# Expert rows on their way to the tokens: plain f32 in two column halves in place of f32r high and low parts

## What is computed

```python
def expert_block(args):
    tok, gte, e = args
    xb = x_pad[tok]
    hb = jax.nn.silu(xb @ w1[e]) * (xb @ w3[e])
    return (hb @ w2[e]) * gte[:, None]
...
y = jnp.zeros((n + 1, d)).at[slot_tok].add(y_slots.reshape(n_slots, d))
```

## Time and profile before

| | us |
|---|---|
| median of 3 runs | 1051.43 (1050.07 to 1052.33) |
| the profiled execution | 1051.55 |
| its span, first to last instruction | 1049.8 |
| PE busy | 997.7 (95%) |
| DVE busy | 503.1 (48%) |
| ACT busy | 343.2 (33%) |
| chain that ended last | PE 75%, DMA 13%, DVE 6% |
| HBM read | 259.60 MB |

### The profile page before, as it was taken

The page is one execution under the profiler, slowest core; times in us unless marked ns, Lnnn a source line. Parts: engine busy times, 40 slices in busy tenths (PEclk is TensorE's granted clock), DMA queues, the critical chain, the costliest instruction groups (busy, mean ns, idle before and its releaser), DMA issues.

```text
span 1049.8 us, 12592 instructions
## 1 busy us (share of the span) xinstructions
PE 997.7 (95%) x4901; PEld 629.3 (60%) x4901; DVE 503.1 (48%) x915; ACT 343.2 (33%) x684; POOL 41.9 (4%) x59
## 2 busy tenths in 40 slices
PE   8999999999999999999997999999999889898894
PEld 7778867766778889877786344444343333333342
DVE  5369799765466445532336333333332232333236
ACT  6442365667763245443232211111111110111113
POOL 1000000000000000000000100000000000000001
PEclk9999999999999999999997999999999999999998
DMA  8422312112113626322278999999999999999992
GB/s 238 130 81 81 120 41 81 41 42 80 41 45 117 234 87 198 123 81 86 73 327 312 381 429 426 427 427 426 426 426 425 429 425 429 425 428 426 426 406 90
DMA packets 64431, 260.72 MB, mean 248 GB/s; under 512 B 11329, under 2 KB 39026, under 8 KB 50802
## 3 DMA queue, kind: packets, MB, share of 16 engines
q1 hardware_dynamic: 59954, 248.08, 59.6%
q0 software_dynamic: 3104, 7.35, 1.9%
q10 hardware_dynamic: 1312, 4.46, 1.2%
HBM read 259.60 MB, written 4.19 MB: 251 GB/s over the span
## 4 chain that ended last, share of the span: by engine, by line
PE 75%; DMA 13%; DVE 6%; issue 3%; ACT 1%; SPq 0%; DVEq 0%; POOLq 0%
PE ps L1958 16%; DMA eraw<-in_w 12%; PE ps L1649 12%; PE ps L1650 12%; PE ps L1651 12%; PE ps L2011 8%; PE ps L2022 2%; PE ps L2023 2%; PE ps L1884 1%; PE ps L1906 1%; PE ps L1826 1%; PE ps L1834 1%; DVE s L1273 1%; DVE nmax L1275 1%; PE ps L1852 1%
## 5 line engine op out<-in xcount | busy, mean ns | idle before, releaser
L1958 PE MATMUL ps<-eraw,XT 128*64 128x512 f32 x992 | 225.9, 598 | 12.8 <-DMA eraw<-in_w 11.6
L1224 DVE TENSOR_TENSOR wlo<-raw,whi 128x2048 fp32r<-128x2048 f32 (+2 forms) x43 | 95.9, 2230 | 115.6 <-ACT whi L906 115.5
L1958 PEld LDWEIGHTS ps<-eraw,XT 128*64 128x64 f32 x992 | 67.4, 136 | 133.7 <-issue 129.5
L2011 PE MATMUL ps<-eraw,HT 128*64 128x512 f32 x512 | 113.0, 593 | 8.2 <-issue 8.2
L1518 DVE TENSOR_TENSOR h<-ps,h 128x512 f32<-128x512 f32 x128 | 79.4, 684 | 82.8 <-PE ps L2023 82.8
L1649 PE MATMUL ps<-xT_hi,whi 128*128 128x512 f32 (+1 forms) x256 | 104.0, 406 | 1.6 <-DVE xT_lo L1231 1.6
L1650 PE MATMUL ps<-xT_lo,whi 128*128 128x512 f32 (+1 forms) x256 | 100.0, 391 | 0.0
L1651 PE MATMUL ps<-xT_hi,wlo 128*128 128x512 f32 (+1 forms) x256 | 100.0, 390 | 0.0
L906 ACT ACTIVATE whi<-raw 128x2048 fp32r<-128x2048 f32 (+2 forms) x43 | 80.1, 1864 | 45.5 <-PE ps L1651 45.3
L2011 PEld LDWEIGHTS ps<-eraw,HT 128*64 128x64 f32 x512 | 39.4, 137 | 79.9 <-issue 79.9
L1064 ACT ACTIVATE HT<-ps 128x512 f32<-128x512 f32 x15 | 9.0, 598 | 197.7 <-PE ps L1996 197.7
(11 more groups left out here) (316 smaller groups left out, 1577.4 us busy)
## 6 DMA issues: line engine op xcount, KB each, us to landing
eraw<-in_w SPq DMA_DIRECT2D x82, 2048.0 KB, 29.1
eraw<-in_w SPq DMA_DIRECT2D x28, 1024.0 KB, 10.8
raw<-in_w_in SPq DMA_DIRECT2D x9, 1024.0 KB, 5.2
raw<-in_w_gate SPq DMA_DIRECT2D x8, 1024.0 KB, 5.4
raw<-in_w_ckv SPq DMA_DIRECT2D x8, 1024.0 KB, 5.3
raw<-in_w_out SPq DMA_DIRECT2D x4, 1024.0 KB, 5.2
raw<-in_w_cq SPq DMA_DIRECT2D x4, 1024.0 KB, 5.1
raw<-in_w_co SPq DMA_DIRECT2D x4, 1024.0 KB, 5.0
```

The source lines that it names most:

```text
L1224: dve.tensor_tensor(wlo[n % 2][:, 0:w], raw[n % RING][:, 0:w], whi[n % 2][:, 0:w].bitcast(f32), ALU.subtract).then_inc(w_lo, 1)
L1958: ins = pe.matmul(ps[1 + c // 2][rows, :], XT[p % 2][:, kk, rows], eraw[slot][:, first + 512 * k:first + 512 * k + 512], start=(kk == 0), ...
L2011: ins = pe.matmul(ps[4 + n][rows, :], HT[:, ff, rows], eraw[slot][:, first + D * f + 512 * n:first + D * f + 512 * n + 512], start=(ff == ...
```

## The change

`Yh` and `Yl` give way to one tile `Y` in f32, and S becomes f32 as well. ACT's copy of the two banks writes `Y`; DVE's subtraction `rest` goes. A combine becomes two plain f32 matmuls: the first takes the stationary columns of tokens 0 to 63 of the tile and writes partitions 0 to 63 of the bank, the second tokens 64 to 127 and partitions 64 to 127; both stream the same 512 columns of `Y`. PE's waits for `yl_kept` become waits for `y_kept`, which ACT raises. In the branch for experts with too many tokens DVE gets a wait for `y_kept`.

```diff
-    Yh = at("Yh", [P, D], f32r, R_C)
-    Yl = at("Yl", [P, D], f32r, R_C, 32 * KB)
-    S = at("S", [P, SEQ], f32r, R_C, 39 * KB)
+    Y = at("Y", [P, D], f32, R_C)
+    S = at("S", [P, SEQ], f32, R_C, 39 * KB)
...
-                    act.activation(Yh[:, 512 * n:512 * n + 512], ps[4 + n][:, :], ACT.Copy).then_inc(yh_kept, 1)
+                    act.activation(Y[:, 512 * n:512 * n + 512], ps[4 + n][:, :], ACT.Copy).then_inc(y_kept, 1)
...
-            def rest(p):
-                for n in (0, 1):
-                    dve.wait_ge(yh_kept, 2 * p + n + 1)
-                    c = slice(512 * n, 512 * n + 512)
-                    dve.tensor_tensor(Yl[:, c], ps[4 + n][:, :], Yh[:, c].bitcast(f32), ALU.subtract).then_inc(yl_kept, 1)
...
-                if p:
-                    rest(p - 1)
...
-            rest(NPAIR - 1)
...
             def combine(t, n, bank):
-                o = ps[bank][:, :]
                 c = slice(512 * n, 512 * n + 512)
-                pe.matmul(o, S[:, P * t:P * t + P], Yh[:, c], start=True, stop=False)
-                pe.matmul(o, S[:, P * t:P * t + P], Yl[:, c], start=False, stop=True).then_inc(comb_made, 1)
+
+                for half in (0, 1):
+                    rows = slice(P // 2 * half, P // 2 * half + P // 2)
+                    ins = pe.matmul(ps[bank][rows, :], S[:, P * t + P // 2 * half:P * t + P // 2 * half + P // 2], Y[:, c],
+                                    start=True, stop=True)
+                ins.then_inc(comb_made, 1)
...
-                pe.wait_ge(yl_kept, 2 * p + 2)
+                pe.wait_ge(y_kept, 2 * p + 2)
...
-                pe.wait_ge(yl_kept, 2 * (NPAIR - 1) + n + 1)
+                pe.wait_ge(y_kept, 2 * (NPAIR - 1) + n + 1)
```

More of the change, by code:

```diff
@@ L501, in build @@
     sg_done, gg_done, h_done, turned, ht_kept = sem("sg_done"), sem("gg_done"), sem("h_done"), sem("turned"), sem("ht_kept")
-    y_half, yh_kept, yl_kept, s_done = sem("y_half"), sem("yh_kept"), sem("yl_kept"), sem("s_done")
+    y_half, y_kept, s_done = sem("y_half"), sem("y_kept"), sem("s_done")
     comb_made, comb_added = sem("comb_made"), sem("comb_added")
@@ L1502, in owned @@
                 dve.wait_ge(s_done, 2 * p + 1)
-                dve.scalar_tensor_tensor(S[:, :], slot_row[:, 1, :], slots, S[:, :].bitcast(f32),
+                dve.scalar_tensor_tensor(S[:, :], slot_row[:, 1, :], slots, S[:, :],
                                          ALU.is_equal, ALU.add).then_inc(s_done, 1)
-            def rest(p):
-                for n in (0, 1):
-                    dve.wait_ge(yh_kept, 2 * p + n + 1)
-                    c = slice(512 * n, 512 * n + 512)
-                    dve.tensor_tensor(Yl[:, c], ps[4 + n][:, :], Yh[:, c].bitcast(f32), ALU.subtract).then_inc(yl_kept, 1)
             def add_one(no, t, n, bank):
@@ L1574, in far_link @@
                     dve.wait_ge(over_chain, far_links[0])
+                dve.wait_ge(y_kept, 2 * NPAIR)
                 dve.wait_ge(comb_added, NC * (NPAIR - 1))
```

## The result

The changed kernel takes 1067.97 us (median of 4 runs, 1066.6 to 1069.26) against 1051.87 us before (4 runs): a ratio of 1.0159, 95% interval 1.0145 to 1.0173, 16.1 us slower. The forecast was 1068.7 us, 0.7 above the median.

The account below looks back on a forecast made before the run. PE was taken to set the pace throughout, the weight loads' 18.5 us lead keeping it from running dry. 12.75 (pairs) + 3.0 (last pair) + 1.4 (end) = 17.15 us on 1051.55 gave 1068.7 us, range 1064 to 1077.

Parts of the forecast that it names:

- The price of a combine: PE's combines: two plain f32 matmuls, 4 records, 0.859 us each; a pair's eight take 6.87 us in place of 4.08.
- The entries: 0.15 us once per stretch of 64-column records after full-array work on PE; two of four a pair go, 0.30 us off.
- The pair and the 14 pairs: PE's time of a pair goes from 27.07 to 29.56 us; down projection of pair 14 ends 12.75 us later.
- The last pair and the end: Last pair's two stretches of combines cost +3.0 us; last eight combines and adds +1.4, the bound moving from DVE to PE.
- the pairs up to 774 us had no wait to fill: Explanation of +12.75 us: later added PE work replaces waits for weights; earlier pairs have none, so their loss stays.
- A later release of weight places: Weight loads: places freed later delay loads that have 18.5 us of lead; put at nothing.
- A: Rival: the loads hide it all; only last pair and end cost, +4.4 us, 1055.9 us; chance 0.04.
- B: Rival: both halves share one stream of Y, a combine costs 0.43 us; -1.2 us, 1050.4 us; chance 0.03.
- C: Rival: the halves run one after the other, a combine costs 1.72 us; 1178.6 us; chance 0.04.
- D: Upper bound as a case: entries stay everywhere, a pair takes 30.15 us; 1077.4 us; chance 0.07 with what lies between.

Follow-up runs that it names:

- e1: Changed kernel with each combine as one whole plain f32 matmul over all 128 columns, no halves; 1078.9 us, ratio 1.0257 to the kernel before.
- e11: Kernel before with the new combine (plain f32, two halves, no low part) in pairs 3 to 9 only; 1051.4 us, ratio 0.9995.
- e5: Kernel before with the new combine (plain f32, two halves, no low part) in pairs 0 to 6 only; 1054.2 us, ratio 1.003.
- e3: Kernel before with the low parts left out: one f32r matmul a combine, no subtraction on DVE; 1050.0 us, ratio 0.998.
- e9: Kernel before with the new combine in pairs 0 to 11, f32r parts in 12 to 15; 1058.7 us, ratio 1.0065.
- e8: Changed kernel with half 0 made twice in place of half 0 and half 1; 1178.0 us, ratio 1.1196 to the kernel before.
- e4: Kernel before with the new combine (plain f32, two halves, no low part) in pairs 7 to 15 only; 1058.4 us, ratio 1.0066.
- e10: Changed kernel with half 0 of four tiles, then half 1 of the same four; 1114.8 us, ratio 1.0596 to the kernel before.

## Why the prediction was right

**The price of a combine.** The 6.87 us for the 32 records of a pair's combines was taken from the down projection; measured are two stretches of 3.43, 6.86. The record count came from 512 records for 256 matmuls, and the combine line has x512.

**The entries.** Two of four entries were to go, 0.30 us a pair. The ups behind combines went from 1.87 to 1.72 and from 3.58 to 3.43, 0.15 each. e1 brought them back together with one of 0.2 in front of each stretch of combines, and the pair went to 30.23. The Trainium skill's rule (TensorEngine Tiling (Array Packing), Key Properties), by which a change of tiling mode drains the engine, agrees with these numbers.

**The pair and the 14 pairs.** Expected 29.56 and 413.84 us, measured 29.53 and 413.46. In the profiled execution down 14 ended at 1025.72, the forecast to the digit, which is luck: the experts began 0.38 us later in it (605.39 against 605.01) and the pairs gave 0.38 back. Term for term: the start +0.38, the pairs +12.37 (+12.75 expected).

**The last pair and the end.** From down 14 to the end of the last down projection 21.68 us (1025.72 to 1047.40), before 18.61 (1012.97 to 1031.58): +3.07, expected 3.0. Besides the stretches and the ups it holds two terms that the sum left out and that leave 0.1 us together: the transposes behind the second stretch take 0.37 in place of 0.22, since they now follow 64-column work, and the last down projection 7.02 in place of 7.07. From there to the end of the span 19.60 us (1067.0), before 18.22 (1049.8): +1.38, expected 1.4. The bound moved as foretold; the timeline of the changed kernel shows adds that each wait for PE:

```profile
1052.60 0.69 DVE L1510 TENSOR_TENSOR h<-ps,h 128x512 f32<-128x512 f32 x1 [0.17 <-PE ps L2015]
1053.46 0.69 DVE L1510 TENSOR_TENSOR h<-ps,h 128x512 f32<-128x512 f32 x1 [0.17 <-PE ps L2015]
```

One add per 0.86 us, where the earlier trace rows had eight in 4.88.

**A sentence that was wrong.** "... the pairs up to 774 us had no wait to fill, and that is what doesn't come back." e11 lengthened seven pairs from 684 us on, three of them in the time in which the kernel before has PE alone on the chain, and nothing was lost; e5 lost 1.5 us of 17 on its chain (2.8 in the median), behind gaps in the loads. It is no matter of where PE waited before. PE's work and the loads are two chains from about 600 us on; each has its own sum (14 x 29.53 against 401), and the later one is the result. The 14 pairs cost 12.4 us because their added 34 us (14 x 2.46) exceed what PE waited in all, 401.1 - 14 x 27.07 = 22.1. The prediction's sum was that of the two chains, and only its explanation was not.

**A part put at nothing that isn't quite nothing.** "A later release of weight places delays loads that have 18.5 us of lead." It does delay them: 421 and 417 GB/s in the first 100 us of the changed kernel, and e5 pays for it. In the changed kernel it costs nothing, since the loads are the earlier chain by some 10 us (413.5 less 401.1 and the 1.9 us that 421 and 417 in place of 427 GB/s come to).

**The rivals.** A would need a combine under 0.745 us; it is 0.86. e3 (25.23 us of PE a pair) and e11 (28.30 on average) lie below the 28.65 us a pair of that point and take the loads' time; e9 (29.18 on average) lies above it and takes PE's. B fell with the 3.43 of the stretch: one shared stream of Y gives nothing beyond the two halves side by side. The Trainium skill's up to 2x (TensorEngine Tiling (Array Packing), Theoretical Speedup) agrees with e8, which has no partner and costs twice; it was already spent in the 0.86. C did not occur, as the halves alternate. D is nearly e1 (1078.9 against 1077.4).

No kernel of this study beats the one before by more than the measurement can tell with all of its computation in place. What PE could save in the 14 pairs is hidden by the loads' 401 us, as e3 shows; what is left is some 2 us in the last pair and at the end.

## What to carry to other kernels

Where an engine and a stream of loads run side by side over a long stage, add up each chain over the whole stage and take the later; the waits that the profile shows at one place don't say what added work costs there. Here 17 us of added work in the middle cost nothing, as the sum of all waits was 22 us. Two places were not free: work behind the last wait (1.5 us in e4), and work at the start, where the slower release of full places stopped the loads for a moment (e5). The price of a new matmul is best taken from a line of the same shape, with its records counted against the code's matmuls and with the entry that each change of tile shape costs. Two column halves pay only side by side: keep them next to each other in the program, or two apart at most.

## What the runs showed that was not expected

PE starts matmuls out of program order across the column halves: with four tiles' first halves in a row the following ups began 1.28 us before combines that stand ahead of them (650.62 and 651.90 in e10), and with two in a row nothing but 0.05 us a stretch was lost (3.48 against 3.43). The reach ends between two and four matmuls of one half in a row (plain f32, 512 columns): at four a stretch takes 4.9 us, and 5.35 where no up can start early. Which of queue length, weight loads or waits ends it was not tried.
